# Moving the key and variance sums, their logarithms and the row loads in the RWKV-7 core of a two-block model

## The reference

```python
kk = heads(k * k_k)
kk = kk / jnp.maximum(jnp.sqrt(jnp.sum(kk * kk, axis=-1, keepdims=True)), 1e-12)
k = k * (1.0 + (a - 1.0) * k_a)
decay = jnp.exp(-jnp.exp(w.astype(f32)))
y = rwkv7_scan(rh, heads(decay), kh, vh, -kk, kk * ah)
    # per token: sa = S a;  S = S*w + sa b^T + v k^T;  y = S r
mean = jnp.mean(y, axis=-1, keepdims=True)
var = jnp.mean(jnp.square(y - mean), axis=-1, keepdims=True)
yn = ((y - mean) * lax.rsqrt(var + RW_GN_EPS)).reshape(B, T, D)
yn = yn * ln_w.astype(f32) + ln_b.astype(f32)
bonus = jnp.sum(rh * kh * r_k.astype(f32), axis=-1, keepdims=True) * vh
out = (yn + bonus.reshape(B, T, D)).astype(x.dtype) * g
```

## Time and profile before

| | us |
|---|---|
| median of 3 runs | 3706.24 (3705.42 to 3706.66) |
| profiled execution, its own time | 3705.42 |
| its span, first to last instruction | 3703.6 |
| PE busy | 3521.9 (95%) |
| DVE busy | 1999.3 (54%) |
| ACT busy | 1226.9 (33%) |
| POOL busy | 1582.5 (43%) |

### The profile page before, as it was taken

How to read it: one execution, slowest core, us unless ns; L and a number is a source line. 1 busy time by engine, 2 the same in 40 slices (tenths; PEclk the granted TensorE clock), 3 DMA queues, 4 the chain that set the end, 5 groups by cost and what they waited for, 6 DMA issues and landing times. The chain is left out here.

```text
span 3703.6 us, 61631 instructions
## 1 busy us (share of the span) xinstructions
PE 3521.9 (95%) x25217; PEld 2773.3 (75%) x25217; DVE 1999.3 (54%) x2415; ACT 1226.9 (33%) x1623; POOL 1582.5 (43%) x1150
## 2 busy tenths in 40 slices
PE   7998999999999889998899879999999999999989
PEld 5876778888888568777778757888888877774667
DVE  6886555554234661216767546555542446858342
ACT  4553333332112562225565423333311131232321
POOL 3432387773333133333433314877733332560242
PEclk9998999999999999999999989999999999999999
DMA  2110022224311132231212021222242112211211
GB/s 99 45 54 31 34 91 79 79 85 142 101 51 45 40 151 91 91 114 70 64 61 83 26 86 40 88 82 85 79 149 88 54 40 92 75 52 40 91 45 74
DMA packets 74495, 276.67 MB, mean 75 GB/s; under 512 B 8256, under 2 KB 8640, under 8 KB 73792
## 3 DMA queue, kind: packets, MB, share of 16 engines
q1 hardware_dynamic: 68544, 252.89, 19.9%
q10 hardware_dynamic: 5760, 20.97, 1.4%
HBM read 208.82 MB, written 65.01 MB: 74 GB/s over the span
## 5 line engine op out<-in xcount | busy, mean ns | idle before, releaser
L117 POOL TENSOR_TENSOR gap<-ones 128x1 f32<-128x1 f32 x152 | 41.8, 275 | 1346.6 <-PE ps L150 879.2
L120 POOL TENSOR_TENSOR wlo<-wraw,whi 128x1024 fp32r<-128x1024 f32 (+3 forms) x152 | 396.9, 2611 | 12.7
L150 PE MATMUL ps<-xh,whi 128*128 128x512 f32 x832 | 269.7, 406 | 31.5 <-DVE xl L1862 10.0
L150 PE MATMUL ps<-xl,whi 128*128 128x512 f32 x832 | 263.8, 398 | 0.0
L150 PE MATMUL ps<-xh,wlo 128*128 128x512 f32 x832 | 263.4, 398 | 0.0
L870 DVE TENSOR_TENSOR h<-ps,h 128x1024 f32<-128x1024 f32 (+1 forms) x56 | 68.5, 1224 | 314.5 <-PE ps L399 275.9
L150 PEld LDWEIGHTS ps<-xh,whi 128*128 128x128 f32 x832 | 155.8, 191 | 83.7 <-DVE xl L1862 12.2
L984 POOL TENSOR_TENSOR wlo<-wraw,whi 128x512 fp32r<-128x512 f32 x126 | 165.5, 1329 | 62.8 <-ACT whi L1107 62.7
L150 PEld LDWEIGHTS ps<-xl,whi 128*128 128x128 f32 x832 | 158.3, 190 | 38.2
L150 PEld LDWEIGHTS ps<-xh,wlo 128*128 128x128 f32 x832 | 158.0, 190 | 38.2
L118 POOL TENSOR_SCALAR whi<-wraw 128x1024 fp32r<-128x1024 f32 (+3 forms) x152 | 179.4, 1180 | 0.0
(11 more groups left out here) (622 smaller groups left out, 9401.1 us busy)
## 6 DMA issues: line engine op xcount, KB each, us to landing
wraw<-w_ffn_in SPq DMA_DIRECT2D x88, 512.0 KB, 3.5
ffn_hidden<-sum_of_squares SPq DMA_DIRECT2D x44, 512.0 KB, 2.6
rw_next<-rw_kept SPq DMA_DIRECT2D x40, 512.0 KB, 5.2
wraw<-w_ffn_out SPq DMA_DIRECT2D x32, 512.0 KB, 3.7
ffn_stage<-ffn_hidden SPq DMA_DIRECT2D x30, 512.0 KB, 4.9
rw_kept<-rw_stage SPq DMA_DIRECT2D x24, 512.0 KB, 2.6
rw_kept<-rw_stage ACTq DMA_DIRECT2D x24, 512.0 KB, 2.7
wraw<-w_ple SPq DMA_DIRECT2D x16, 640.0 KB, 3.8
```

The source lines that it names most:

```text
L117: nc.gpsimd.tensor_tensor(g.gap[:, 0:1], g.ones[:, 0:1], g.ones[:, 0:1], ALU.mult)
L120: nc.gpsimd.tensor_tensor(g.wlo[:, s, 0:w], g.wraw[:, s, 0:w], g.whi[:, s, 0:w].bitcast(F32), ALU.subtract).then_inc(g.w_split.sem, 1)
L150: last = nc.tensor.matmul(acc[:, hf, :], w[:, s, c:c + P], x[:, kt, hf * HALF:(hf + 1) * HALF], start=start and kt == 0 and n == 0, stop=s ...
```

## The change

Only the order of the instructions in `rw_core` changes; none is added or removed. Line numbers after the place of the first hunk are 7 lower in the changed kernel.

```diff
-                def load_receiver(m):
+                def load_rest(m):
                     sp.wait_ge(g.prep_ready.sem, g.prep_ready.base + m)
                     sp.dma_start(r, g.rw_tile[RW_R][m]).then_inc(g.rv_loaded.sem, 16)
-
-                def load_value(m):
                     sp.wait_ge(g.tr_done.sem, g.tr_done.base + NT * m)
                     sp.dma_start(v, g.rw_tile[RW_V][m]).then_inc(g.rv_loaded.sem, 16)
...
                 for m in range(KD):
-                    sp.wait_ge(g.tr_done.sem, g.tr_done.base + NT * m + 1)
                     if m + 1 < KD:
                         load_first(m + 1)
-                        load_receiver(m + 1)
-                    if m > 1:
-                        store(m - 2)
-                        gate(m - 1)
-                    if m + 1 < KD:
-                        load_value(m + 1)
-                store(KD - 2)
-                gate(KD - 1)
+                        load_rest(m + 1)
+                    if m:
+                        store(m - 1)
+                        gate(m)
                 store(KD - 1)
...
-                    inverses(m, 1, 0)
+                    for h in (0, 1):
+                        inverses(m, 1, h)
                     if following:
                         pe.wait_ge(g.w_ready.sem, g.w_ready.base + 2 * m + 2)
                         key_sum(m + 1)
-                    inverses(m, 1, 1)
+                    for h in (0, 1):
+                        corrections(m, 2, h)
                     if prior:
                         variance(m - 1)
-                    for h in (0, 1):
-                        corrections(m, 2, h)
...
                         squares(m - 1)
+                    keep_correction(m, 2, 0)
                     if following:
                         log_key(m + 1)
+                    keep_correction(m, 2, 1)
                     if prior:
                         log_variance(m - 1)
-                    keep_correction(m, 2, 0)
-                    keep_correction(m, 2, 1)
+                    keep_correction(m, 3, 0)
                     if following:
                         inverse_key(m + 1)
-                    keep_correction(m, 3, 0)
                     keep_correction(m, 3, 1)
...
                     grow(m, 2, 1)
+                    grow(m, 3, 0)
                     if following:
                         unit_key(m + 1)
-                    grow(m, 3, 0)
                     grow(m, 3, 1)
```

## The result

The change makes the kernel slower: 3746.36 us, the median of 4 runs (3745.13 to 3750.60), against 3705.83 of the kernel before beside it. The ratio is 1.0111, 95% interval 1.0096 to 1.0127, or 40.5 us. The forecast of 3724 had the direction, and less than half of the size: it expected 18.2 us, and the time lies 8 us above the upper end of its range.

A forecast was written before the change was run, and what follows sets the result against it. PE was taken as the bound, with the doubling setting `solutions`. Pass 0 4.2, six passes 13.8, pass 7 0.2 and SP 0 sum to 18.2 us on the median of 3706.24: forecast 3724, range 3711 to 3738.

The forecast's parts named there:

- What bounds the kernel: PE is busy 95% of the span; the doubling sets when `solutions` starts, and its shift once per pass is the effect.
- Part 1, the timetable: PE, ACT and DVE steps of pass 2, replayed in the new order: `solutions` 2.3 us later, 13.8 over six passes.
- the large term: Level 3: the copy for h = 1 waits behind table load and exponential, 2.15 us of delay.
- Part 1, the durations behind the pause: Level 3's second inverse and the steps up to `solutions`, priced at durations of before; that inverse 1824.75 to 1825.8.
- The clock as a rival: Near `solutions`: longer pauses double the slow-clock stretch, 1.7 us in each of 8 passes, 13.6, giving 3738; chance 0.12.
- Pass 0: First pass, with no variance to cover the logarithm: `solutions` 4.4 us later, taken as 4.2.
- Part 2, SP: SP's queue: first loads leave 3.8 us earlier, their reader, DVE's scan, doesn't wait on a DMA; effect 0.
- The gaps: Rival: PE's 9.4 us of instruction stalls in the outputs get hidden by the longer doubling pauses, 3715; chance 0.11.
- dearer switch: Rival: ACT's table switch waits for a copy to drain, 0.48 twice in 7 passes, 3731; chance 0.03.
- SP's queue is late: Rival: loads land late and the scan waits for a DMA, 3.4 us in 6 passes, 3744; chance 0.03.
- Faster: Rival: level 2's corrections start 1.3 us earlier and 7 passes keep it, minus 9.1, 3697; chance 0.05.
- passes that differ by more than the clock explains: Sign that the prediction is wrong: passes of the changed kernel differing among each other beyond the clock's effect.

The follow-up runs named there:

- exp_only: The kernel before with only the key's exponential moved behind the first copy of level 3, and `unit_key` behind `grow`: 3733.78 us, ratio 1.0066.
- ln_only: The kernel before with only the logarithms moved, the key's between the two copies of level 2, the variance's behind them: 3743.20 us, ratio 1.0090.
- the pair of filled kernels: Unread matmuls in PE's pauses, added to the change without SP's part (3725.78 us, 1.0050) and to the kernel before (3693.12 us, 0.9967).
- order_only: The changed kernel with SP's code of before, so the change on PE, ACT and DVE only: 3738.71 us, ratio 1.0079 to the kernel before.
- order_busy: `order_only` with 178 matmuls that nobody reads added in PE's pauses in the last part of the doubling: 3725.78 us, ratio 1.0050 to the kernel before.
- sp_only: The kernel before with the change's hunks on SP alone, loads no longer waiting for the first transposes: 3717.02 us, ratio 1.0020.

## Why the prediction was right or wrong

**What bounds the kernel.** Right. `solutions` is set by the doubling, and what moved the time acts through PE.

**Part 1, the timetable.** Right until the pause in level 3. With 12.11 added, the steps of pass 2 come at 1822.41 (measured 1822.40) for the second inverse of level 1, 1823.46 (1823.45) for the key sum, 1829.41 (1829.27) and 1830.66 (1830.59) for level 2's inverses, 1835.96 (1835.76) for the copy behind the exponential, and 1836.86 (1836.65) for level 3's second inverse. Level 2's corrections start 3.0 us behind the second copy of level 1, as forecast. That level 3's exponential was the large term is borne out by `exp_only`; that the logarithm alone would cost as much (`ln_only`) I had not seen.

**Part 1, the durations behind the pause.** This is the step that failed. I put "inverse of level 3, h = 1, 1824.75 to 1825.8", that is 1.05 us, and everything behind it at the prices that the kernel before has at full clock. It took 1.92, and the rest of the pass up to `solutions` ran at half speed, so `solutions` starts at 1843.14 instead of 1841.76. The 2.3 a pass are about what the order costs at full clock: the pair of filled kernels shows 2.27 in passes 1 and 2, less in two others. The forecast's 18.2 are then some 18 of the 29 us of `order_only`, although no run shows its 4.2 for pass 0 at full clock. The other 11 go with the slow stretches: PE is at half speed for 133.1 us in `order_only` against 78.5, and `order_busy`, at full clock in passes 1, 2, 5 and 6, got back 11 to 13. This is no clean subtraction, since the fillers also take away the slow stretch that the kernel before has (3.4 us in its pass 2), and since passes 0, 3 and 4 stayed slow.

**The clock as a rival.** The right mechanism, mis-sized, with a chance of 0.12. I let the slow stretch double, from 3.4 to 6.8 us a pass, for 1.7 us. It became 9.4 us in pass 2, and 167.3 against 78.5 us over the eight passes and the work just behind them, 88.8 more instead of 8 x 3.4 = 27. The order alone has 54.6 more, twice the 27, and its 3738.7 us are the rival's 3738 all the same; that match is luck. What I held against the rival, that the pause in level 3 might only move the slow stretch, fell: level 3 and the last level have pauses of their own, and the stretch now covers all of them and `solutions` too.

**Pass 0.** 4.2 predicted, 12.9 measured (67.16 against 54.25). The doubling has 7.6 of it: the uncovered logarithm makes the pause that I wrote down, 2.04 us before level 2's second inverse, and behind it the corrections of level 3 take 3.54 instead of 2.06. Another 3.8 (11.64 against 7.84 from the outputs to the gram) are SP's, since `order_only` has 7.66 there. The other 1.5 are spread over the rest of the pass.

**Part 2, SP.** This is the second step that failed. The times were right: the loads of the pass leave at 1795.03, where those of before, at 1786.98 plus 12.11, would leave at 1799.09. And the scan didn't wait. The term 0 was wrong nonetheless, 7 us by `sp_only`. I looked for who reads the loaded data late, and the loads hurt somebody who doesn't read them: PE, whose issue waits grew. The earlier trace rows had a sign of it, a wait for "issue" in the outputs, into which the loads of pass 0 moved. I used it only for a rival on the other side, in which pauses would hide it.

**The other rivals.** The gaps took nothing back: 9.8 us in `order_only` against 9.4, and 15.7 with SP's part. No dearer switch: the table load runs 1.28 us with the function directly behind it, in the new place as in the old. "SP's queue is late" asked for a scan that waits, which it doesn't. Faster: level 2's inverses came 0.5 late by the shifted times, not early.

**Left open.** About 4 us of the whole change that neither part shows alone, and why the clock falls where it does. In pass 4 of the changed kernel too it falls before level 3's pause, at 1958.6, behind pauses of at most 0.20 us in the 10 us before, as in passes 3 and 4 of `order_busy`; in passes 1, 2, 3, 5 and 6 it falls at or just behind that pause. The prediction's warning, passes that differ by more than the clock explains, was triggered in part: passes 4 and 5 have the same clock, 0.89, and take 61.73 and 63.64 us, and the difference lies between the outputs and the next `gram` (6.39 against 9.04), where PE has its issue waits. Pass 6 (66.89 us, clock 0.82) I have not followed further.

## What to carry to other kernels

- A pause of PE costs its length and also what it does to the work that follows it: read the durations of the matmuls behind every pause in the trace, and price the work behind a new pause at full and at half clock before choosing one.
- Before a transfer is moved to an earlier time, look at which engine works there with many small instructions; its "issue" waits are ones that the transfer can lengthen, even where its data are read in good time.
- Where a chain between engines leaves pauses on PE that can't be removed, cheap matmuls that nobody reads may pay: here a dozen short ones per pass, 0.33%. Measure them pass by pass, since 14 in one place took 1.70 us at full clock and 3.17, more than the pause, where the clock had already fallen.

## What the runs showed of the hardware

- After a pause of 1.8 to 2.0 us on PE in level 3, which came behind a dense stretch, 32 matmuls took 1.92 us instead of 1.12, and the mean granted clock over the 10 us around and behind the pause was 0.53 to 0.60. 14 matmuls of 128x256 in bf16, 1.70 us, put in that pause kept it at 1.00 in pass 2 of `order_busy`. Such a pause isn't needed for the clock to fall: in passes 3 and 4 of that kernel it fell with no pause over 0.20 us in the 10 us before. The 88.8 more microseconds at 1.2 GHz would add 44.4 if PE bound all of them; its busy time grew by 31.8.
- With the DMA engines 96% busy just before, PE stood still for 3.25 us ("issue" in the profile) in pass 0 of `sp_only`, where the same place of the kernel before, without those transfers, had 0.50.
